# A hybrid decoder block on eight cores: compress reads k/v by phase, norm tails cross block ends, selection masks land in chunks, gates move into the query stage

## The reference, cut to what matters

```python
h = rms_norm(x, norm_mix);  z = h @ w_in
q, kc, vc, ksl, vsl, kw, vw, g, u = split(z)
def compress(kv, pos, w1, w2):             # 127 overlapping blocks: 32 tokens long, stride 16
    blocks = kv[:, 16 * c + l] + pos[l]    # c = 0..126, l = 0..31
    return silu(blocks.reshape(..., 32 * 128) @ w1) @ w2
k_cmp = rms_norm(compress(kc, ...), k_norm_cmp);  v_cmp = compress(vc, ...)
o_cmp, p_cmp = compressed_attention(q, k_cmp, v_cmp)
sel = top16 of 32 blocks of 64 tokens, by p_cmp, shared in a group
o_slc = selected_attention(q, rms_norm(ksl), vsl, sel)
o_win = window_attention(q, rms_norm(kw), vw)
gates = sigmoid(g + gate_b)                # one number per head and branch
o_nsa = gates[0] * o_cmp + gates[1] * o_slc + gates[2] * o_win
```

## Time and profile before

| what | value |
|---|---|
| median of three runs | 2099.95 us (2077.18 to 2152.7) |
| the profiled execution | 2081.65 us |
| its slowest core, number 6, first to last instruction | 2080.6 us |
| the other cores | 2064.5 to 2076.1 us |
| PE busy on core 6 | 1836.6 us, 88% of the span |
| ACT, DVE busy | 528.7 us (25%), 823.8 us (40%) |
| stages on core 6: keys and values / queries / gates and compress / attention / rest | 0 to 258 / to 326 / to 377 / to 704 / to 2081 us |

### The profile page before, as it was taken

How to read it: one execution, slowest core, us unless ns; L and a number is a source line. 1 busy time by engine, 2 the same in 40 slices (tenths; PEclk the granted TensorE clock), 3 DMA queues, 4 the chain that set the end, 5 groups by cost and what they waited for, 6 DMA issues and landing times.

```text
span 2080.6 us, 30098 instructions; the slowest of 8 cores (2064.5 to 2080.6 us)
## 1 busy us (share of the span) xinstructions
PE 1836.6 (88%) x10841; PEld 1005.7 (48%) x11010; DVE 823.8 (40%) x1565; ACT 528.7 (25%) x929; POOL 126.8 (6%) x129
## 2 busy tenths in 40 slices
PE   3799987898997798499577799999999999999999
PEld 2455534566664343388433444444444444444444
DVE  3333111364664667322537340432423404314234
ACT  3233143477776423300342200000000000000000
POOL 1100100000000000000000000001001000010000
PEclk9999996899999999699698899999999999999999
DMA  9721874332435000595222029449277294492753
GB/s 210 130 82 41 90 77 52 64 42 43 68 47 80 3 1 0 156 174 88 29 41 41 12 30 122 57 65 118 33 93 90 33 121 62 60 122 34 89 81 162
DMA packets 187216, 153.13 MB, mean 74 GB/s; under 512 B 12992, under 2 KB 176448, under 8 KB 182720
## 3 DMA queue, kind: packets, MB, share of 16 engines
q0 software_dynamic: 173968, 107.13, 41.7%
q1 hardware_dynamic: 13104, 44.07, 6.8%
HBM read 249.78 MB, written 8.52 MB: 124 GB/s over the span
## 4 chain that ended last, share of the span: by engine, by line
PE 80%; DVE 6%; another core or an unknown queue 4%; DMA 4%; ACT 3%; issue 3%; POOL 1%; DVEq 0%; ACTq 0%; SPq 0%; POOLq 0%
PE pair L1226 15%; PE bank L1228 15%; PE bank L1243 7%; PE pair L1243 7%; PE pair L521 5%; PE bank L521 4%; DMA arena<-sel 3%; PE bank L1099 3%; PE pair L1099 3%; PE pair L1028 3%; PE bank L1028 3%; PE pair L757 3%; PE bank L924 2%; PE bank L919 2%
## 5 line engine op out<-in xcount | busy, mean ns | idle before, releaser
L1226 PE MATMUL pair<-arena 128*128 128x512 bf16 x1380 | 316.6, 380 | 1.6 <-issue 0.2
L1228 PE MATMUL bank<-arena 128*128 128x512 bf16 x1380 | 316.0, 379 | 1.5
L1231 DVE TENSOR_TENSOR arena<-bank,arena 128x512 bf16<-128x512 f32 x88 | 60.9, 692 | 547.9 <-PE pair L1226 411.2
L1230 ACT ACTIVATE arena<-pair 128x512 bf16<-128x512 f32 x88 | 52.5, 597 | 823.9 <-PE pair L1226 823.9
L746 ACT ACTIVATE arena<-bank,arena 128x512 bf16<-128x512 f32 (+3 forms) x402 | 215.3, 573 | 80.2 <-PE bank L736 28.6
L1226 PEld LDWEIGHTS pair<-arena 128*128 128x128 bf16 x1408 | 138.0, 98 | 166.7 <-issue 1.4
L1228 PEld LDWEIGHTS bank<-arena 128*128 128x128 bf16 x1408 | 137.8, 98 | 166.1
L1243 PE MATMUL pair<-arena 128*128 128x512 bf16 x699 | 166.0, 379 | 0.3
L1243 PE MATMUL bank<-arena 128*128 128x512 bf16 x680 | 163.9, 379 | 1.3
L469 PE MATMUL bank<-arena 128*128 128x128 bf16 x544 | 54.6, 280 | 115.2 <-DVE arena L461 115.2
L757 PE MATMUL pair<-arena 128*128 128x129 bf16 (+1 forms) x1184 | 121.9, 223 | 25.7 <-DVE arena L750 22.5
(11 more groups left out here) (163 smaller groups left out, 1883.7 us busy)
## 6 DMA issues: line engine op xcount, KB each, us to landing
arena<-xc SPq DMA_DIRECT2D x24, 1024.0 KB, 10.0
arena<-w_gate POOLq DMA_DIRECT2D x22, 1024.0 KB, 16.3
arena<-w_up POOLq DMA_DIRECT2D x22, 1024.0 KB, 18.6
arena<-w_down POOLq DMA_DIRECT2D x22, 1024.0 KB, 13.3
arena<-w_in POOLq DMA_DIRECT2D x18, 1024.0 KB, 13.2
arena<-w_out POOLq DMA_DIRECT2D x8, 1024.0 KB, 32.1
y<-arena SPq DMA_DIRECT2D x8, 1024.0 KB, 4.0
arena<-sel SPq DMA_DIRECT2D x4, 1024.0 KB, 9.0
```

Of the source, the lines that this page charges most:

```text
L1226: op(PE, lambda: nc.tensor.matmul(bank[pg][:, :], lhsT=wgt[:, kc, cc * 128:(cc + 1) * 128], rhs=h3T[:, kc, tc * 512:(tc + 1) * 512], start ...
L1228: op(PE, lambda: nc.tensor.matmul(bank[pu][:, :], lhsT=wut[:, kc, cc * 128:(cc + 1) * 128], rhs=h3T[:, kc, tc * 512:(tc + 1) * 512], start ...
```

## The change

`kcvcT` becomes `[128, 4, 16, 128]`: token `16c + r` lies at phase `r`, position `c`. The copy out of PSUM that fills it reads PSUM at a stride of 16 and writes runs of 32. Both groups of a kind are then read by one matmul of 254 columns, two contiguous runs of 127. Silu is written as tanh with two DVE operations, and one norm serves both groups. `proj_tm` also flushes; the flushes at block ends are gone but for one ahead of compress. The gate tiles are interleaved in the query stage and use Exp and a DVE reciprocal. `u_proj` is started in compress: `pump` takes 8 + 8 + 16 + 24 = 56 of its matmuls there, and the stream goes on with what is left (`fill`). The mask is read in chunks of four key tiles, each with two DMAs of 64 partitions and a buffer of its own.

```diff
         def proj_tm(...):
...
+            flush(0)
             return psi
...
-        kcvcT = self.tile(CK, "kcvcT", [128, 4, TC], BF16)
+        kcvcT = self.tile(CK, "kcvcT", [128, 4, 16, 128], BF16)
...
-                        copy_op(evac_engine(), kcvcT[:, idx, tg:tg + 512], bank[psi][:, :], ...)
+                        copy_op(evac_engine(), kcvcT[:, idx, :, q_ * 32:(q_ + 1) * 32], bank[psi][:, :].rearrange("p (c r) -> p r c", r=16), ...)
...
-                flush(0)                       # end of a ksl or kw block
...
-            flush(0)                           # end of a quarter
...
                     pnorm(psi, 512, eps[:, 2:3], [epsb], qnT[:, h, tc * 512:(tc + 1) * 512], qnTb[h][tc])
-            flush(0)
+                    if tc == 0:
+                        gate_tile(h)           # 16 matmuls of 24 columns, DVE add
+            if blk == 3:
+                op(ACT, ... AF.Exp, scale=-1.0)   # gates, all 192 columns
+                op(DVE, ... + 1.0)
+                op(DVE, ... reciprocal)
             wrel()
-        for tt in range(8):
-            (16 matmuls of 24 columns, DVE add, ACT Sigmoid)
...
+        w1s = [wget(), wget()]
+        fill = u_proj()
+        flush(0)
         for kind in range(2):
...
             for l in range(32):
                 op(PE, ... matmul(bank[pbi][:, 0:1], lhsT=w1[:, l, :], rhs=posbf[...]))
+                if l % 4 == 3:
+                    pump(1)
...
-            for g in range(2):
-                src = kcvcT[:, kind * 2 + g, :]
-                for l in range(32):
-                    op(PE, ... matmul(bank[psi][:, 0:127], lhsT=w1[:, l, :], rhs=src[:, l:l + 16 * 126 + 1:16]))
-                op(ACT, ... Silu);  second matmul;  norm and flush(0), or copy
+            for l in range(32):
+                src = kcvcT[:, 2 * kind:2 * kind + 2, l % 16, l // 16:l // 16 + 127]
+                op(PE, ... matmul(bank[psi][:, 0:254], lhsT=w1[:, l, :], rhs=src))
+            op(ACT, ... Tanh, scale=0.5);  op(DVE, ... x / 2);  op(DVE, ... (tanh + 1) * x / 2)
+        second matmul of k, ACT Square;  pump(16);  second matmuls of v;  ones-matmul, ACT Ln, Exp;  pump(24);  DVE multiply
...
-                for hf in range(2):
-                    dma(SP, Em[64 * hf:64 * hf + 64, 0:nt, :], src, r=[seldb[n]], w=[Emb] + Emdb if hf == 0 else [], pw=[Emb] + Emdb if hf else [], owner=Emb)
+                for c in range(nt // 4):
+                    bs = Emdb if c == nt // 4 - 1 else [Emb[c]]
+                    for hf in range(2):
+                        dma(SP, Em[64 * hf:64 * hf + 64, 4 * c:4 * c + 4, :], src, r=[seldb[n]], w=bs if hf == 0 else [], pw=bs if hf else [], owner=bs[0])
...
-        run_stream(all_jobs(), NPTS - 1, u_proj())
+        run_stream(all_jobs(), NPTS - 1, fill)
```

More of the change, by code:

```diff
@@ L636, in build @@
                     pnorm(psi, 512, eps[:, 2:3], [epsb], qnT[:, h, tc * 512:(tc + 1) * 512], qnTb[h][tc])
-            flush(0)
-            wrel()
-        gtmp = self.tile(P1, "gtmp", [128, 24], F32)
-        gtmpb = self.buf("gtmp")
-        for tt in range(8):
-            psi = rot_proj.next()
-            for kc in range(16):
-                op(PE, lambda: nc.tensor.matmul(bank[psi][:, 0:24], lhsT=hT[:, kc, 32 + tt * 128:160 + tt * 128], rhs=wg[:, kc, :], start=(kc == 0), stop=(kc == 15)), r=[wgb, hTb[tt // 4]], w=[bankb[psi]])
-            op(DVE, lambda: nc.vector.tensor_tensor(out=gtmp[:, :], in0=bank[psi][:, 0:24], in1=pvec[:, PV_GB:PV_GB + 24], op=ALU.add), r=[bankb[psi], pvb], w=[gtmpb])
-            op(ACT, lambda: nc.scalar.activation(out=gates[:, tt, :], in_=gtmp[:, :], func=AF.Sigmoid), r=[gtmpb], pw=[gatesb])
@@ L663, in build @@
[L663 to L664 removed]
+        posbb = [self.buf(f"posb{j}") for j in range(2)]
+        th = [self.tile(C1, f"th{j}", [128, 256], F32) for j in range(2)]
+        thb = [self.buf(f"th{j}") for j in range(2)]
+        xh = [self.tile(C1, f"xh{j}", [128, 256], F32) for j in range(2)]
+        xhb = [self.buf(f"xh{j}") for j in range(2)]
+        h1 = [self.tile(C1, f"h1_{j}", [128, 256], BF16) for j in range(2)]
@@ new lines, in build @@
+        wrel(2)
+        pk = rot_proj.next()
+        op(PE, lambda: nc.tensor.matmul(bank[pk][:, 0:254], lhsT=w2[:, 0, :], rhs=h1[0][:, 0:254], start=True, stop=True), r=[w2b, h1b[0]], w=[bankb[pk]])
+        op(ACT, lambda: nc.scalar.activation(out=sqt[0][:, 0:254], in_=bank[pk][:, 0:254], func=AF.Square), r=[bankb[pk]], w=[sqtb[0]])
+        pump(16)
+        for g in range(2):
+            pv_ = rot_proj.next()
+            op(PE, lambda: nc.tensor.matmul(bank[pv_][0:127, 0:128], lhsT=h1[1][:, 127 * g:127 * g + 127], rhs=w2[:, 1, :], start=True, stop=True), r=[w2b, h1b[1]], w=[bankb[pv_]])
+            copy_op(DVE, vcaug[0:127, g, 0:128], bank[pv_][0:127, 0:128], r=[bankb[pv_]], pw=[vcaugb])
@@ new lines, in build @@
+        si = rot_ssq.next()
+        op(PE, lambda: nc.tensor.matmul(bank[si][:, 0:254], lhsT=ones, rhs=sqt[0][:, 0:254], start=True, stop=True), r=[sqtb[0], cidb], w=[bankb[si]])
+        op(ACT, lambda: nc.scalar.activation(out=th[0][:, 0:254], in_=bank[si][:, 0:254], func=AF.Ln, scale=1.0 / DH, bias=eps[:, 0:1]), r=[bankb[si], epsb], w=[thb[0]])
+        op(ACT, lambda: nc.scalar.activation(out=th[0][:, 0:254], in_=th[0][:, 0:254], func=AF.Exp, scale=-0.5), w=[thb[0]])
+        pump(24)
+        op(DVE, lambda: nc.vector.scalar_tensor_tensor(out=kcmpT[:, :, 0:127], in0=bank[pk][:, 0:254].rearrange("p (g c) -> p g c", g=2), scalar=pvec[:, PV_KNC:PV_KNC + 1], in1=th[0][:, 0:254].rearrange("p (g c) -> p g c", g=2), op0=ALU.mult, op1=ALU.mult), r=[bankb[pk], thb[0], pvb], pw=[kcmpb])
@@ L687, in build @@
         C1.close()
[L688 removed]
+        self.free(posbb + h1b + thb + xhb)
         CK.close()
```

119 lines of the change are left out of this document (59 added, 60 removed).

## The result

| what | before | after |
|---|---|---|
| median | 2077.88 us | 2024.76 us |
| all executions | 2077.18 to 2152.7 (5) | 2020.75 to 2107.27 (5) |
| ratio (the 2099.95 us execution counted in; without it 0.974) | | 0.971 [0.963, 0.979] |
| profiled execution, its slowest core's span | 2081.65, 2080.6 (core 6) | 2024.76, 2023.5 (core 7) |

The forecast was 2016 us in a range of 1992 to 2046. Of the changed kernel 2020.75, 2022.93 and 2024.76 us remain, 2022.9 in the middle. Every time given for an experiment is the middle one of its executions (the mean of the middle two of an even number), and "longer" or "shorter" without more is against these 2022.9 us.

A forecast was written before the change was run, and what follows sets the result against it. PE, busy 88%, was taken to lose time at norm tails, gates, slow strided compress and mask waits. Terms 13.0 + 12.3 + 20.9 + 3.5 + 16 = 65.7 us off 2081.65 gave 2016 us, range 1992 to 2046.

The forecast's parts named there:

- Tails in the key and value stage: Key and value blocks: second norm tail goes behind 16 more matmuls, six PE waits of about 2.2 us go, 13.0 us.
- no new wait, by a margin of half a microsecond: Key and value stage: banks come free 2.8 us behind a tail's ones-matmul, and the tightest place allows over 3 us.
- Query stage and gates: Query stage: three of four tail waits go (6.6 us), gates interleaved between projections save 5.7 us; together 12.3 us.
- Compress: Compress stage: 19.7 us at mostly full clock replace 40.6, a gain of 20.9 us, bounds about 0 and 22.5.
- twice by the clock, twice by the read: Compress: a strided column costs four times a contiguous one, 1.73 against 0.42 ns, split evenly between these two factors.
- The rival with the low clock in compress: Compress stays at the low clock, and the gain at attention's start is lost too: 2033 us, chance 0.12.
- Strided copies: Copies out of PSUM at a stride of 16: ACT and DVE have idle time, nothing reaches PE, 0 us.
- Start of attention: First 6.6 us of attention shrink to about 2.5 plus 0.6 for ACT: 3.5 us gained, bounds 0 and 4.5.
- Filler used up earlier: Attention: 56 fewer filler matmuls left; heads take 12.0 us with filler, 12.1 without, so moving it gives 0.
- Masks: Attention passes: chunked mask DMAs let first tiles start earlier; some 3 of 21.1 us waiting remain, 16 us taken.
- the masks gain nothing: Rival: the mask wait only moves from a pass's first tile to its ninth or thirteenth; 2032 us, chance 0.18.
- Everything lands well: Rival: no mask waits, no clock loss in compress, slow stretches behind mask waits go; 2003 us, chance 0.10.

The follow-up runs named there:

- The early memset: Changed kernel with w2v in a buffer record of its own, so POOL's memset runs early: 2015.4 us; together with free mask halves 1993.6 us.
- free mask halves: Changed kernel with a buffer record for each half of each mask chunk, so no half waits in SP's queue for the other: 2008.1 us, 0.967.
- The strided experiment: Changed kernel with the phase layout alone undone: 254 columns a matmul, read with a step of 16 elements: 2051.8 us, 0.988.
- 127 columns to a matmul: Kernel before with the phase layout alone: contiguous columns of one group per matmul, as many matmuls as before: 2064.4 us, 0.994.
- the load early: Changed kernel with the loads of biasT and bonus issued ahead of the query stage instead of at the start of attention: 2021.0 us, 0.973.
- the first experiment: Changed kernel with the masks of a pass again in two whole DMAs instead of chunks: 2035.6 us, 0.981 of the kernel before.

## Why the prediction was right, and where not

*Tails in the key and value stage (13.0; measured 14.7 to 15.6).* The six waits went as counted. Two errors of opposite sign nearly cancel, which is luck. The three later quarters gained 18.4 us on the slowest core, 12.6 of them waits; the sum left out the stretches at the lower clock behind these. Core 6 of the kernel before has 10.2 us at 0.50 there, in three windows (columns as in the windows above):

```profile
130.80:134.20 3.40, 3.18 (x9) 1.16 (x9) 2.78 (x3) 2.91 (x5) 0.00 (x0) 0.50 0.00 0
182.00:185.40 3.40, 3.40 (x21) 2.31 (x20) 1.55 (x3) 2.93 (x3) 0.00 (x0) 0.50 0.01 2
233.20:236.60 3.40, 3.24 (x9) 1.18 (x8) 0.75 (x1) 1.06 (x2) 0.00 (x0) 0.50 1.26 143
```

At half the speed that is some 5 us. The changed kernel has none in these quarters. Four cores of the kernel before have one such stretch, and gained 15.1. And "no new wait, by a margin of half a microsecond" failed, in the first quarter. The margin was worked out for banks behind a tail that DVE takes up at once; there DVE stood still behind the memset, by three steps. The rows for it were in the earlier trace rows, and the step "PE arrives earlier only to wait longer" used them for PE alone, without asking what else would stand behind the same memset once the tail's multiply came later in DVE's queue. PE's wait there grew from 6.25 to 14.46 us, by 8 where about 4 had been foreseen. The early memset shows what the whole wait is worth: 12.4 us to the queries' start, 14.5 to the kernel's end with free mask halves.

*Query stage and gates (12.3; 13.4).* Right by its steps; the last wait stayed at 2.19 us, no gate tile waited, and undoing the gates' part costs 5.5 us in this stage and compress where 5.7 had been taken. The 1.1 us more are open.

*Compress (20.9; 23.1).* Right in size, and its largest term by a wrong reason. The prediction read "twice by the clock, twice by the read". The strided experiment shows that the clock has no part in a strided column: 1.80 ns at 1.00 and at 0.50, and the kernel before has the same 0.23 us for 127 columns. Contiguous columns do go with the clock, 0.43 ns at 1.00 and 0.84 at 0.50 (107 ns for 127). So the layout had to come first: a higher clock alone would have given the strided reads nothing. The sum survived because the change takes away both. The 1.6 us added for a stretch at the lower clock were one case of two: five cores have none (17.4 us), the three others lost 1.6 to 1.9 us to it.

The rival with the low clock in compress fell: 1.00 on the slowest core. What it said of the clock for the whole stage is seen with strided reads (0.50), for most of it with 127 columns to a matmul (0.68), and in a small part with the gates behind the query stage (0.86).

*Strided copies (0).* Right: 692 ns before and 691 after on DVE, 585 and 586 on ACT. The Trainium skill's sentence on PSUM lines (SBUF — State Buffer, Door 1: The DMA port swizzle), which speaks of matmuls, doesn't carry over to these copies; its rule on SBUF lines agrees with the 1.80 ns against 0.43 ns a column.

*Start of attention (3.5; a loss of 0.9 to 2.3).* The failed step is "another 0.6 until ACT has caught up". What ACT waits for was read from the rows of before, where a load had 6.6 us of cover by slow matmuls. The change took the cover away, and nothing of the prediction asked what had been under it. With the load early the stretch takes 19.7 us on the median core, 3.1 less than before: nearly the 3.5 that had been forecast.

*Filler used up earlier (0).* Taken from the earlier trace rows, which show selected heads alone. From its mask write to the convolution, pass 3 has 10 filler matmuls left where it had 60, and is 2.2 us shorter on the median core though its masked tiles wait only 0.3 us less. With whole masks it is still 1.7 us shorter than before, though these tiles wait 0.9 us longer. So moving the filler seems to have given some 2 us there; no run changes it alone.

*Masks (16; 11.9 on the median core, 5.7 on the slowest).* The mechanism was right, and its sizes in part: in pass 1 a DMA took 3.5 to 5.1 us (3.2 taken), a step from chunk to chunk 4.3 to 5.1 us (4.9 taken), the last chunk landed 23.4 us behind the first issue (21.1 taken). What was too low is the rest of waiting. It put 3 us for all, and 9.4 to 10.6 us are left on six cores, 7.4 on one, 18.0 on the slowest: the last chunk came 2.3 us later than taken in pass 1, and from its landing to PE's matmul another 1.4 us pass (446.55 to 447.93). Against this, the stage gained more than its waits: on core 5 they fell by 6.8 of 12.0 us. Its passes 0 and 1 (71.6 and 84.7 us before) went from a clock of 0.98 to 1.00, some 3 us more, which the forecast had only in its rival of all going well; the other 2 us lie in pass 3, where the filler is gone. The Trainium skill's rule on batching DMAs (DMA: Bandwidth & Descriptors, Bandwidth) does not decide here. The last byte does land later in chunks, as the forecast drew from it (in pass 1 on core 0 24.1 us behind the mask write, 17.4 with whole masks), but the kernel is shorter: in a chain, whole masks take 12.7 us more than chunks of 256 KB (2035.6 and 2022.9), and without a chain 15.8 more (2023.9 and 2008.1). "SP has nothing else queued there" was true and missed the point, since what it queues behind is itself. And one reading of the old rows was off: the second mask DMA did not take about as long as the first in pass 0 (5.95 against 8.87 us); no term rests on it.

*The sum.* 65.7 us forecast, 57.1 measured on the slowest cores and 58 between the median cores; the three terms ahead of attention gave 6 us more than forecast, attention 15 less on the slowest core. That 2022.9 lies so near 2016 owes something to these opposite errors. The likeliest case held, and of the rivals "the masks gain nothing" fell with the first experiment. "Everything lands well" put the kernel at 2003 us by its sum; free mask halves alone bring 2008.1, and with the early memset, which it didn't have in view, 1989 to 1994 are measured.

## What to carry to other kernels

Where a change lets an engine arrive earlier at a wait, write down everything that stands behind the same releaser on the other engines' queues: here a memset held a copy, the copy a DVE step, and that step a bank. Loads that were hidden by a slow stage come to light when the stage gets fast; look for what is issued in the stretch that shrinks. Here a transfer cut into chunks gained its full worth only when the chunks were issued without waiting for each other.

## What the runs showed of the hardware

A matmul whose moving columns lie 32 bytes apart advances by 1.80 ns a column, at a granted clock of 1.00 and of 0.50 alike (0.457 us for 254 columns); contiguous ones take 0.43 ns at 1.00 (109 ns for 254) and 0.84 ns at 0.50 (107 ns for 127). During the strided chain the clock went from 1.00 to 0.50 with PE counted busy in every microsecond, so a busy PE in the profile doesn't mean that the clock holds. Copies out of PSUM at a stride of 64 bytes took no longer on ACT and DVE (586 and 691 ns). Six mask DMAs of 256 KB issued at once take 3.6 to 6.5 us each and have landed 12.0 us behind the mask write (core 0, pass 0); issued in their chain, 3.4 to 4.3 us each, 19.4 us behind it.
